# Attention mixer: fp32 operands in one matmul instead of three, and second Fourier step, pool projection and the first output products inside the attention's steps

## The chip, the cores and the metric

One core of one Trainium2 chip. The metric is the device time of one execution in microseconds (us). Engines are named as in the profile: PE is the matmul engine (PEld its weight loads), DVE the vector engine, ACT the scalar engine, POOL the GpSimd engine, SP the engine that issues the weight transfers.

## The reference, cut to what matters

Two blocks run one after the other on x of 512 tokens by 1024 channels. The first block has two layers of feed-forward, mixer, feed-forward; the change touches only its mixer:

```
p = rmsnorm(x) @ w_in[l]                 # 2048 columns: a 256, f 256, q 512, k 512, v 512
y_pool = pool_mixer(a, pool_w, pool_scale)          # window means, then a 64x64 product per group
y_four = real(fft2(f)) @ fourier_w                  # over 64 channels, then over 512 tokens
for each of 4 heads and both halves j of 64 channels:
    s = q_j k_j^T / 8 - slope * |i - t|;  p_j = softmax(s)
o = (p_0 - lam * p_1) @ v;  y_attn = rmsnorm(o over the head's 128) * (1 - lam_init)
x = x + concat(y_pool, y_four, y_attn) @ w_out
```

The second block (memory, block and dilated attention) is not touched.

## The kernel before

**Products.** Activations lie feature-major in SBUF (128 channels by 512 tokens a tile). A product of fp32 data is made from split operands: `x_hi` is x rounded to fp32r, `x_lo` the rest, and the helper `three` issues hi*hi, hi*lo and lo*hi as three fp32r matmuls (lines 439 to 441). Plain fp32 matmuls stand in a few places only, such as the means over channels (L459, L659) and the transposes (L640).

**Weights.** All weights come as panels of 128x2048 through two slots. SP loads `raw`, ACT writes `w_hi` in two halves (L888, `split`), POOL writes `w_lo` in four quarters (L431), and PE waits in `panel(p)`. ACT may only split panel p+2 when PE is done with panel p (`split_after(p, s)`), so a panel that follows a short one comes late.

**The mixer, first stage.** `MIX_ORDER` lists 24 "units", each one PSUM bank of 128x512: a, f, q, fc (first Fourier step, over channels), k, yf (second Fourier step, over tokens, two panels, 48 matmuls), v, four (the Fourier weights), pool. A unit goes through four banks in turn; PE waits in `free_bank(i)` until unit i-4 is out. Every unit is read by ACT (`unit_hi`) and by DVE (`unit_lo`); for a, f, q, k, v DVE first multiplies by the reciprocal norm into `hraw`, then ACT makes the hi part, then DVE the lo part. On ACT the same loop also holds the panel splits, in the order of the units. `pool_block` (DVE) stands ahead of q 2 and of k 1. The vectors fc share their tiles with v.

**The mixer, attention.** 16 pairs (head h, block b of 128 queries) run through a software pipeline; the loop counts steps s:

- PE in step s: scores of s (halves j=0 and j=1 on rows 0 to 63 and 64 to 127 of the array, into bank pair `2 * (s % 2) + j`), transposes of s-3, every second step the outputs of two pairs (v times at), each fourth step the sum for the head norm (L659).
- ACT in step s: in some steps the square of a head's output, or the `guesses` for its norm (a table load, three operations; the next Exp loads its table again), then Exp of s, sometimes the next head's bias, then `at_hi` of s-3 (L1067).
- DVE in step s: bias and maximum of s (L1467, then `nmx` L1471, which releases `s_max`), the combination `att` of s-1 (L1477 to L1482), `at_lo` of s-3 (L1264), and for four steps the head norm (`newton`, L1495, L1498, L1264).

After the last step come the output products: `project_out` goes through 4 panels with two output tiles each (j, g), 8 contraction tiles k each, and waits for head k-4 at k >= 4 of the first. Its results go to x on DVE (L1317), and the second feed-forward begins.

## Time and profile before

| | |
|---|---|
| median of 3 runs | 2718.3 us (2717.61 to 2718.39) |
| the profiled execution | 2716.47 us, of which the span of its instructions is 2714.5 |
| PE busy | 2507.8 us, 92% of the span |
| DVE, ACT, POOL busy | 1259.7, 1108.5, 1116.9 us |
| granted TensorE clock, mean | 0.966 of full |

The shares are means over stages that differ: the page's slices show PE at 9 or 10 tenths in the feed-forwards and at 6 or 7 in the slices of the two mixers. A row of the timeline gives start (us), duration (us), engine, line, operation, output<-inputs, shape, count, and in brackets the idle time ahead of it and who ended it. A row of the windows gives the stretch, its length, then for each engine the busy us and in parentheses the instructions, then the granted clock of TensorE (0.50 is 1.2 GHz, 1.00 is 2.4 GHz), the share of the DMA engines and GB/s.

### The profile page before, as it was taken

The numbers are of one execution on the slowest core, as the hardware profiler recorded it, in microseconds if no ns is written. First come the engines' busy times: TensorE is split into PE (matmuls) and PEld (weight loads), VectorE is DVE, ScalarE is ACT, GpSimd is POOL, SyncE is SP. The second block draws the span as 40 slices with busy tenths as digits, with TensorE's granted clock in tenths as the row PEclk, the third lists the DMA queues.
The fourth block names the chain that finished last, engine by engine and source line by source line (L and its number), as shares of the span: only waits on it lengthen the run. The fifth ranks groups of instructions, "written<-read, shape, count | busy, mean of one in ns | idle before, by whom it ended". The sixth has DMA issues, their size and how long they took to land.

```text
span 2714.5 us, 31002 instructions
## 1 busy us (share of the span) xinstructions
PE 2507.8 (92%) x11290; PEld 2011.8 (74%) x11290; DVE 1259.7 (46%) x2005; ACT 1108.5 (41%) x1616; POOL 1116.9 (41%) x828
## 2 busy tenths in 40 slices
PE   6999999769999999999999589999999997899977
PEld 5888787547888788887887367887887675777756
DVE  5444025563444115443044745444067756566662
ACT  4333133453333224332143534332146665456662
POOL 4455445304545445544445114554443231433222
PEclk9999999879999999999999789999999998999999
DMA  3222222202222222222223002222232221122211
GB/s 147 97 102 93 93 99 102 93 1 78 95 106 93 93 93 93 93 98 96 97 103 114 33 32 93 93 93 93 93 140 74 74 78 39 69 95 64 77 55 62
DMA packets 37470, 233.25 MB, mean 86 GB/s; under 512 B 5632, under 2 KB 5632, under 8 KB 10624
## 3 DMA queue, kind: packets, MB, share of 16 engines
q1 hardware_dynamic: 35424, 224.42, 23.7%
q10 hardware_dynamic: 1952, 7.54, 0.7%
q8 instruction: 63, 1.03, 0.2%
q14 instruction: 31, 0.25, 0.0%
HBM read 223.55 MB, written 2.10 MB: 83 GB/s over the span
## 4 chain that ended last, share of the span: by engine, by line
issue 61%; POOL 38%; POOLq 1%
POOL w_lo L431 38%; POOLq L425 0%; POOLq L429 0%; POOLq L202 0%; POOLq L431 0%; POOLq L1823 0%
## 5 line engine op out<-in xcount | busy, mean ns | idle before, releaser
L431 POOL TENSOR_TENSOR w_lo<-raw,w_hi 128x512 fp32r<-128x512 f32 x824 | 1116.7, 1387 | 1597.1 <-ACT w_hi L888 1596.8
L439 PE MATMUL ps<-h_hi,w_hi 128*128 128x512 f32 x2304 | 924.5, 401 | 36.9 <-DVE h_lo L1264 15.0
L441 PE MATMUL ps<-h_hi,w_lo 128*128 128x512 f32 x2304 | 904.6, 393 | 0.0
L440 PE MATMUL ps<-h_lo,w_hi 128*128 128x512 f32 x2304 | 904.5, 393 | 0.0
L888 ACT ACTIVATE w_hi<-raw 128x1024 fp32r<-128x1024 f32 x412 | 413.5, 1052 | 862.9 <-PE ps L441 855.3
L439 PEld LDWEIGHTS ps<-h_hi,w_hi 128*128 128x128 f32 x2304 | 438.1, 190 | 136.5 <-issue 18.6
L440 PEld LDWEIGHTS ps<-h_lo,w_hi 128*128 128x128 f32 x2304 | 438.4, 190 | 93.3 <-issue 5.3
L441 PEld LDWEIGHTS ps<-h_hi,w_lo 128*128 128x128 f32 x2304 | 437.1, 190 | 93.4
L439 PE MATMUL ps<-hid_hi,w_hi 128*128 128x512 f32 x704 | 279.6, 397 | 7.5 <-DVE hid_lo L1264 7.5
L441 PE MATMUL ps<-hid_hi,w_lo 128*128 128x512 f32 x704 | 278.7, 396 | 0.0
L440 PE MATMUL ps<-hid_lo,w_hi 128*128 128x512 f32 x704 | 278.3, 395 | 0.0
L1317 DVE SCALAR_TENSOR_TENSOR x_sb<-ps,x_sb 128x512 f32<-128x512 f32 x64 | 43.6, 686 | 451.1 <-PE ps L441 451.1
L1336 DVE TENSOR_TENSOR sq<-hraw,sq 128x512 f32<-128x512 f32 x88 | 139.7, 1588 | 222.6 <-ACT hraw L975 222.6
L888 ACT ACT_TABLE_LOAD x42 | 53.9, 1283 | 320.3 <-PE ps L441 315.7
L439 PEld LDWEIGHTS ps<-hid_hi,w_hi 128*128 128x128 f32 x704 | 132.6, 188 | 41.0 <-DVE hid_lo L1264 9.2
L1332 DVE TENSOR_TENSOR hraw<-ps,guess 128x512 f32<-128x512 f32 x88 | 60.8, 691 | 213.2 <-PE ps L441 212.4
L441 PEld LDWEIGHTS ps<-hid_hi,w_lo 128*128 128x128 f32 x704 | 132.6, 188 | 32.7
L440 PEld LDWEIGHTS ps<-hid_lo,w_hi 128*128 128x128 f32 x704 | 132.4, 188 | 32.0
L1338 DVE CAST hid_hi<-sq 128x512 f32 (+1 forms) x88 | 111.3, 1264 | 14.7 <-issue 14.5
L1264 DVE TENSOR_TENSOR hid_lo<-sq,hid_hi 128x512 f32 (+1 forms) x88 | 100.6, 1143 | 12.6 <-issue 0.2
L748 PE MATMUL ps<-cst,att 128*128 128x128 f32 x304 | 52.7, 309 | 36.9 <-ACT att L1132 35.0
L1124 ACT ACTIVATE pt_hi<-ps 128x256 fp32r<-128x256 f32 (+2 forms) x64 | 43.2, 675 | 106.6 <-PE ps L748 106.1
(267 smaller groups left out, 2482.5 us busy)
## 6 DMA issues: line engine op xcount, KB each, us to landing
raw<-in_stream SPq DMA_DIRECT2D x206, 1024.0 KB, 4.8
hraw<-xs SPq DMA_DIRECT2D x96, 64.0 KB, 2.0
x_sb<-in_x ACTq DMA_DIRECT2D x1, 2048.0 KB, 10.5
out_x<-x_sb SPq DMA_DIRECT2D x8, 256.0 KB, 2.7
mem_sb<-in_mem ACTq DMA_DIRECT2D x1, 1024.0 KB, 13.3
rec_sb<-in_recip ACTq DMA_DIRECT2D x2, 512.0 KB, 4.7
memn<-in_mem ACTq DMA_DIRECT2D x1, 1024.0 KB, 4.8
dist_sb<-in_dist ACTq DMA_DIRECT2D x2, 448.0 KB, 3.1
```

The lines of the kernel that those rows point to most:

```text
L431: ins = gp.tensor_tensor(w_lo[:, s, c], raw[:, s, c], w_hi[:, s, c].bitcast(F32), ALU.subtract)
L439: pe.matmul(dst, l_hi, r_hi, start=first, stop=False)
L440: pe.matmul(dst, l_hi, r_lo, start=False, stop=False)
L441: return pe.matmul(dst, l_lo, r_hi, start=False, stop=last)
L748: mm = pe.transpose(dst, src, const(C_ID))
L888: act.activation(w_hi[:, s, c], raw[:, s, c], ACT.Copy).then_inc(hi_split, 1)
L1124: act.activation(pt_hi[:, :, 0:kbs, P * b:P * b + P], src, ACT.Copy).then_inc(t_thi, 1)
L1264: return dve.tensor_tensor(dst, src, hi.bitcast(F32), ALU.subtract)
L1317: dve.scalar_tensor_tensor(out=x_sb[:, m, :], in0=ps[:, m, :], scalar=scale, in1=x_sb[:, m, :], op0=ALU.mult, op1=ALU.add).then_inc(x_read ...
L1332: dve.tensor_tensor(hraw[:, e, :], ps[:, 2 * e, :], rstd, ALU.mult).then_inc(gate_in, 1)
L1336: dve.tensor_tensor(sq[:, e, :], hraw[:, e, :], sq[:, e, :], ALU.mult)
L1338: dve.tensor_copy(hid_hi[:, c, :], sq[:, e:e + 1, :])
```

## The change

Queries, keys, values and probabilities stay fp32 and unsplit (`q_sb`, `k_sb`, `v_sb`, `at_sb`): one fp32 matmul stands where three fp32r ones stood, DVE writes q, k and v alone, and `at_lo` is gone. `fc` gets tiles of its own. The order of the stream becomes v ahead of yf, and the units yf, pool, four (20 to 25, `BEFORE1` = 20) leave the first stage: PE does them in pieces at the end of the attention's steps 0 to 11 (`fill`), into banks 2 and 3. For that the scores have one pair of banks (0 and 1) instead of two, and PE waits for the maximum of s-1 ahead of the scores of s. ACT and DVE take the hi and lo part of a finished unit in the step after (6, 8, 9, 10, 11, 12); the splits of panels 11, 12 and 13 of the mixer's stream move into ACT's steps 4, 8 and 12. In steps 16, 17, 18 and 20 `fill` issues the products k = 0 to 6 of the first two output tiles, and `project_out` begins there with k = 7.

The order of the units:

```
-    + [("yf", c, 8 if c else None) for c in range(2)]
-    + [("v", t, 10 if t == 3 else None) for t in range(4)]
-    + [("four", c, None) for c in range(2)]
-    + [("pool", c, 11 if c else None) for c in range(2)]
+    + [("v", t, 8 if t == 3 else None) for t in range(4)]
+    + [("yf", c, 10 if c else None) for c in range(2)]
+    + [("pool", c, None) for c in range(2)]
+    + [("four", c, 11 if c else None) for c in range(2)]
...
+BEFORE1 = 20
+MIX_UNITS = [(kind, c, i % 4 if i < BEFORE1 else 2 + c, ends) for i, (kind, c, ends) in enumerate(MIX_ORDER)]
+
+FILL_STEPS = {5: 20, 7: 21, 8: 22, 9: 23, 10: 24, 11: 25}
```

The matmul engine:

```
+                def yf(e, c, ts):
+                    w = [t[:, e, :].rearrange("p (t n) -> p t n", t=TB) for t in (w_hi, w_lo)]
+                    s = slice(256 * c + P * e, 256 * c + P * e + P)
+                    for t in ts:
+                        mm = three(ps[:, 2 + c, :], fc_hi[:, t, s], fc_lo[:, t, s],
+                                   w[0][:, t, :], w[1][:, t, :], e == 0 and t == 0, e == 1 and t == TB - 1)
+                    return mm
+
+                def fill(s):
+                    if s < 8:
+                        e, c, ts = s // 4, s // 2 % 2, range(2 * (s % 2), 2 * (s % 2) + 2)
+                        if s % 4 == 0:
+                            panel(p0 + 9 + e)
+                        mm = yf(e, c, ts)
+                        if s == 3:
+                            mm.then_inc(panel_done, 1)
+                    elif s < 10:
+                        c = s - 8
+                        if c == 0:
+                            panel(p0 + 11)
+                        pe.wait_ge(unit_lo, lo0 + 21 + c)
+                        pe.wait_ge(pooled, 2 * l + c + 1)
+                        w = slice(512 + P * c, 512 + P * c + P)
+                        mm = three(ps[:, 2 + c, :], w_hi[:, 0, w], w_lo[:, 0, w],
+                                   m_hi[:, c, :], m_lo[:, c, :], True, True)
+                    elif s < 12:
+                        c = s - 10
+                        pe.wait_ge(unit_lo, lo0 + 23 + c)
+                        for k in range(2):
+                            w = slice(256 * k + P * c, 256 * k + P * c + P)
+                            mm = three(ps[:, 2 + c, :], w_hi[:, 0, w], w_lo[:, 0, w],
+                                       f_hi[:, k, :], f_lo[:, k, :], k == 0, k == 1)
+                    elif UNITS1 <= s <= UNITS1 + 4 and s != UNITS1 + 3:
+                        ks = {UNITS1: (0, 1), UNITS1 + 1: (2, 3), UNITS1 + 2: (4, 5), UNITS1 + 4: (6,)}[s]
+                        if s == UNITS1:
+                            panel(p0 + MIX_PANELS)
+                            pe.wait_ge(s_max, u0 + UNITS1)
+                            pe.wait_ge(unit_lo, lo0 + NU)
+                        for k in ks:
+                            if k >= 4:
+                                pe.wait_ge(s_y, HEADS1 * l + k - 3)
+                            for g in range(2):
+                                project(0, g, 1, k, k)
+                    if s in FILL_STEPS:
+                        finish(FILL_STEPS[s], mm)
...
-                        if s >= 2:
-                            pe.wait_ge(s_max, u0 + s - 1)
+                        if s >= 1:
+                            pe.wait_ge(s_max, u0 + s)
                         for j in range(2):
                             r, c = slice(64 * j, 64 * j + 64), slice(P * b, P * b + P)
-                            mm = three(ps[:, 2 * (s % 2) + j, :], q_hi[r, h, c], q_lo[r, h, c],
-                                       k_hi[r, h, :], k_lo[r, h, :], True, True)
+                            mm = pe.matmul(ps[:, j, :], q_sb[r, h, c], k_sb[r, h, :], start=True, stop=True)
...
-                            mm = three(ps[:, 6 + h % 2, q], v_hi[:, kb, c], v_lo[:, kb, c],
-                                       at_hi[:, kb, q], at_lo[:, kb, q], kb == 0, kb == TB - 1)
+                            mm = pe.matmul(ps[:, 6 + h % 2, q], v_sb[:, kb, c], at_sb[:, kb, q],
+                                           start=kb == 0, stop=kb == TB - 1)
...
+                    fill(s)
+                project_out(p0 + MIX_PANELS, 1, lambda k: pe.wait_ge(s_y, HEADS1 * l + k - 3),
+                            begun=(KB - 1, 0, 0, 0))
```

The scalar engine, at the end of its step s:

```
+                    if s - 1 in FILL_STEPS:
+                        i = FILL_STEPS[s - 1]
+                        unit_high(i)
+                        if MIX_UNITS[i][3] is not None:
+                            split_after(p0 + MIX_UNITS[i][3], (MIX_UNITS[i][3] + 1) % 2)
+                    if s == 4:
+                        split_after(p0 + 9, 0)
```

The vector engine, for q and k, and in its step s:

```
+                        ins = dve.scalar_tensor_tensor(out=(q_sb if kind == "q" else k_sb)[:, c, :], in0=src,
+                                                       scalar=0.125 if kind == "q" else 1.0,
+                                                       in1=rstd, op0=ALU.mult, op1=ALU.mult)
...
-                        remainder(at_lo[:, :, q], ps[:, 4 + u % 2, :].rearrange("p (k n) -> p k n", k=TB),
-                                  at_hi[:, :, q]).then_inc(s_tlo, 1)
+                    if s - 1 in FILL_STEPS:
+                        unit_low(FILL_STEPS[s - 1])
```

**ACT in the first stage.** The engine ACT from the first unit q on, before (L1031 is the hi part of a unit, L888 a half of a panel's split):

```order
L1031 ACTIVATE q_hi<-hraw 128x512
L888 ACTIVATE w_hi<-raw 128x1024 x2
L1031 ACTIVATE q_hi<-hraw 128x512 x2
L888 ACTIVATE w_hi<-raw 128x1024 x2
L1031 ACTIVATE q_hi<-hraw 128x512
L1031 ACTIVATE v_hi<-ps 128x512 x3
L888 ACTIVATE w_hi<-raw 128x1024 x2
```

and ACT at the same place now (L903 is the split, L1036 the hi part):

```order
L1036 ACTIVATE f_hi<-hraw 128x512
L903 ACTIVATE w_hi<-raw 128x1024 x4
L1036 ACTIVATE fc_hi<-ps 128x512 x3
L903 ACTIVATE w_hi<-raw 128x1024 x2
L1036 ACTIVATE fc_hi<-ps 128x512
```

The hi parts of q are gone, and with them the place of the second split behind the third q.

**PE in a step of the attention.** The engine PE in step 5, before (L439 to L441 the scores, L640 the transposes):

```order
L439 MATMUL ps<-k_hi,q_hi 128x512
L440 MATMUL ps<-k_lo,q_hi 128x512
L441 MATMUL ps<-k_hi,q_lo 128x512
L439 MATMUL ps<-k_hi,q_hi 128x512
L440 MATMUL ps<-k_lo,q_hi 128x512
L441 MATMUL ps<-k_hi,q_lo 128x512
L640 MATMUL ps<-cst,att 128x128 x4
```

and PE in step 5 now, with the scores, transposes and outputs of step 6 behind it (L646, L654, L665):

```order
L646 MATMUL ps<-k_sb,q_sb 128x512 x2
L654 MATMUL ps<-cst,att 128x128 x4
L440 MATMUL ps<-w_hi,fc_hi 128x512
L441 MATMUL ps<-w_lo,fc_hi 128x512
L442 MATMUL ps<-w_hi,fc_lo 128x512
L440 MATMUL ps<-w_hi,fc_hi 128x512
L441 MATMUL ps<-w_lo,fc_hi 128x512
L442 MATMUL ps<-w_hi,fc_lo 128x512
L646 MATMUL ps<-k_sb,q_sb 128x512 x2
L654 MATMUL ps<-cst,att 128x128 x4
L665 MATMUL ps<-at_sb,v_sb 128x256 x4
```

Six matmuls of the second Fourier step came in behind the transposes, and the next scores stand behind them.

**DVE in a step.** The engine DVE in a step of the attention before, from the maximum on (ISA rows are the maximum's operation and its read):

```order
L1471 TENSOR_SCALAR nmx<-mx 128x2
L1477 RECIPROCAL rsum<-ssum 128x2
L1479 TENSOR_SCALAR att<-prob,rsum 128x512
L1480 TENSOR_TENSOR rsum<-rsum,nlam_all 128x1
L1482 SCALAR_TENSOR_TENSOR att<-prob,rsum,att 128x512
L1264 TENSOR_TENSOR at_lo<-ps,at_hi 128x4x128
```

and DVE in step 6 now:

```order
L1503 TENSOR_SCALAR nmx<-mx 128x2
L1509 RECIPROCAL rsum<-ssum 128x2
L1511 TENSOR_SCALAR att<-prob,rsum 128x512
L1512 TENSOR_TENSOR rsum<-rsum,nlam_all 128x1
L1514 SCALAR_TENSOR_TENSOR att<-prob,rsum,att 128x512
L1283 TENSOR_TENSOR f_lo<-ps,f_hi 128x512
```

At the place of `at_lo`, in six of the steps, stands the lo part of a filled unit; in the others nothing stands there.

## Rows read from the trace of the kernel before

**Rows 1.** Windows: first stage, attention (first layer), two stretches in it, one before.

```profile
394.00:510.60 116.60, 108.27 (x470) 87.66 (x468) 54.09 (x69) 44.11 (x59) 64.67 (x48) 0.97 0.31 108
510.60:608.00 97.40, 62.60 (x285) 42.52 (x285) 68.83 (x196) 53.77 (x108) 4.99 (x4) 0.72 0.06 22
515.00:535.50 20.50, 14.29 (x58) 9.21 (x54) 15.27 (x52) 13.07 (x30) 0.80 (x1) 0.50 0.15 52
535.50:549.10 13.60, 6.23 (x44) 4.23 (x42) 10.56 (x34) 6.94 (x17) 0.00 (x0) 1.00 0.00 1
444.80:450.10 5.30, 5.27 (x12) 4.13 (x13) 0.69 (x1) 1.19 (x2) 4.92 (x4) 0.50 0.58 198
```

**Rows 2.** Timeline, DVE and ACT, one step of the attention and one early step.

```profile
519.27 0.06 DVE L1465 MEMSET tick<- 128x1 f32 x1
522.52 0.06 DVE L1465 MEMSET tick<- 128x1 f32 x1
...
540.34 0.69 DVE L1467 CUSTOM_DVE_ANT_0 prob<-ps,bias 128x512 f32<-128x512 f32 x1
543.36 0.57 ACT L1067 ACTIVATE at_hi<-ps 128x512 fp32r<-128x512 f32 x1
544.58 0.69 DVE L1467 CUSTOM_DVE_ANT_0 prob<-ps,bias 128x512 f32<-128x512 f32 x1
```

**Rows 3.** Timeline, PE: first matmul of yf, of v, of the scores; transposes.

```profile
469.21 0.39 PE L439 MATMUL ps<-w_hi,v_hi 128*128 128x512 f32 x1
481.80 0.40 PE L439 MATMUL ps<-w_hi,h_hi 128*128 128x512 f32 x1
510.62 0.50 PE L439 MATMUL ps<-k_hi,q_hi 64*128 64x512 f32 x2 [1.56 <-DVE h_lo L1452]
540.57 0.63 PE L640 MATMUL ps<-cst,att 128*128 128x128 f32 x4 [1.88 <-DVE at_lo L1264]
```

**Rows 4.** Timeline, ACT and PE, at the panel after fc.

```profile
436.41 0.28 PE L439 MATMUL ps<-w_hi,f_hi 128*128 128x256 f32 x1
438.22 1.99 ACT L888 ACTIVATE w_hi<-raw 128x1024 fp32r<-128x1024 f32 x2
444.83 0.79 PE L439 MATMUL ps<-h_hi,w_hi 128*128 128x512 f32 x1 [1.37 <-POOL w_lo L431]
```

**Rows 5.** Timeline, ACT and DVE, from the end of v to the first maximum.

```profile
503.79 2.01 ACT L888 ACTIVATE w_hi<-raw 128x1024 fp32r<-128x1024 f32 x2 [1.30 <-PE ps L441]
509.68 1.99 ACT L888 ACTIVATE w_hi<-raw 128x1024 fp32r<-128x1024 f32 x2
512.65 0.06 DVE L1465 MEMSET tick<- 128x1 f32 x1 [2.09 <-ACT bias L1038]
```

**Rows 6.** Timeline, DVE: first nmx, a head norm, the last operation of the heads.

```profile
514.09 0.49 DVE L1471 TENSOR_SCALAR nmx<-mx 128x2 f32<-128x2 f32 x1
565.43 0.68 DVE L1257 SCALAR_TENSOR_TENSOR newt<-ms,newt 128x512 f32<-128x512 f32 x1
568.91 0.69 DVE L1467 CUSTOM_DVE_ANT_0 prob<-ps,bias 128x512 f32<-128x512 f32 x1
607.86 0.69 DVE L1264 TENSOR_TENSOR h_lo<-hraw,h_hi 128x512 fp32r<-128x512 f32 x1
```

**Rows 7.** Timeline, ACT: a head's guesses, to the next Exp.

```profile
553.25 1.28 ACT L898 ACT_TABLE_LOAD   x1
557.83 0.72 ACT L1056 ACTIVATE prob<-prob,nmx 128x512 f32<-128x512 f32 x1
```

**Rows 8.** Timeline, PE: an fp32 mean over 512 columns among fp32r matmuls.

```profile
36.30 1.02 PE L459 MATMUL ps<-sq,cst 128*128 128x512 f32 x2
37.40 0.40 PE L440 MATMUL ps<-h_lo,w_hi 128*128 128x512 f32 x1
37.63 0.40 PE L441 MATMUL ps<-h_hi,w_lo 128*128 128x512 f32 x1
```

**Rows 9.** One tile's group: k_lo, nanoseconds min/median/max.

```profile
L1264 DVE TENSOR_TENSOR k_lo<-hraw,k_hi x8: 693/694/1679, 454.5 to 1461.5; 128x512 fp32r<-128x512 f32 x8
```

More of the change, by code:

```diff
@@ L572, in mixer1 @@
                     i = feature_major(i, j)
[L574 to L587 removed]
                 for j in range(2):
[L589 removed]
+                    panel(p0 + 7 + j)
                     w = [t[:, j, :].rearrange("p (k n) -> p k n", k=KB // 2) for t in (w_hi, w_lo)]
@@ L1000, in mixer1, with unit_high @@
                 act.dma_start(rec_sb[:].rearrange("p a n -> p (a n)"), recip).then_inc(in_mix, 16)
[L1001 to L1007 removed]
+                def unit_high(i):
+                    kind, c, bank, ends = MIX_UNITS[i]
                     if kind in NORMED:
@@ L1031, in mixer1 @@
                     act.activation(dst, src, ACT.Copy, scale=scale).then_inc(unit_hi, 1)
-                    if (kind, c) == ("pool", 1):
+                for i in range(BEFORE1):
+                    kind, c, bank, ends = MIX_UNITS[i]
+                    if (kind, c) == ("v", 0):
+                        split_after(p0 + 7, 0)
+                    if ends is not None and (kind, c) != ("a", 1):
                         split_after(p0 + ends, (ends + 1) % 2)
+                    if kind not in WHOLE:
+                        unit_high(i)
                 def head_bias(h):
```

172 lines of the change are left out of this document (62 added, 110 removed).

## The prediction

> **What bounds the kernel now.** I read the page's slices first: the matmul engine is the bound in the feed-forwards and loses its density in two places only, the mixers. The windows then split the first layer's mixer [rows 1]. In the first stage, 116.6 us, PE is busy for 108.3: PE bounds it. In the attention, 97.4 us, PE is busy for 62.6 and at a mean clock of 0.72, while DVE has 68.8. Work that leaves the first stage shortens it at PE's price, and work put into the attention costs nothing as long as the chain of DVE and ACT sets the step. The second layer repeats both stages (the head norms, softmax and splits have the same counts), so I work one layer and double it.
>
> The timeline shows that chain. A late step lasts from the maximum at 540.34 to the next at 544.58, 4.24 us [rows 2]: maximum and nmx (1.4), two Exps, at_hi at 543.36 (0.57), at_lo until 544.58 (0.65). DVE waits in it for ACT. An early step, before any at_lo exists, goes from 519.27 to 522.52, 3.25 us: there DVE alone is the bound. PE is free for half of either.
>
> **Matmuls, price of one.** Two fp32r matmuls of 512 columns start 0.23 us apart at the full clock; a plain fp32 one pushes its successor: from 36.30 to 37.40 lie it and one fp32r, so it takes 0.87 [rows 8]. Three fp32r cost 0.69. Unsplitting therefore does not save PE time, it costs a quarter more. For 256 columns (outputs) I take half, 0.43 against 0.35, an estimate from the same rows. The halves of the scores run side by side on their 64 rows [rows 3] (x2 in 0.50); no row shows this for fp32. I take it as the same (pair about 1.0 us); the other end is one after the other, 1.9. What the unsplit form saves is on DVE and ACT: at_lo, and the lo and hi parts of q, k, v.
>
> **First stage, what goes.**
> - yf, from 481.80 back to 469.21 [rows 3], 12.6 us, with one late panel in it. It moves whole into the steps; v follows k, and its two panels of 48 matmuls (10.9 us) each cover the supply of the next.
> - The panel after fc. ACT's second split begins at 438.22, behind the hi part of a q that waited for the window sums; PE began fc, so was done with that panel, at 436.41 [rows 4]. Now nothing stands ahead of it: 1.6 us earlier at 436.6. PE's two other stalls there go, but it then waits for this panel until 444.83 - 1.6. I take 1.6. Ends: 0, and 4.2 if the low clock behind the gap [rows 1] (last row, 12 matmuls in 5.3 us, half speed) goes as well.
> - From the end of v to the first maximum: 503.79 to 512.65, 8.9 us, today with four and pool in it. Now ACT does one split and the first bias, the same two as from 509.68 to 512.65, 3.0 us [rows 5]; DVE's v 3 and PE's first scores, together some 2 us, go beside it. Saved: 5.9.
>
> Sum: 20.1 us a layer. Into the steps go 66 matmuls of fill, 15 us of PE.
>
> **The steps, from the first nmx (514.09) to the last head's lo part (607.86 + 0.69): 94.5 us now** [rows 6]. Worked interval by interval, first up to the fourteenth nmx:
> - To the third nmx 6.6 as now: the table load of the first Exp sets it.
> - Steps without a fill's lo part are DVE's 3.25 instead of 4.24. PE fits at the full clock: transposes 0.6 [rows 3] and six fill matmuls 1.4 run beside the maximum, the next scores (1.0) beside att. Four such intervals, 13.0.
> - Steps 6, 8, 9, 10, 11, 12 keep the old chain, with a hi part put in (0.53) and the unit's lo in the place of at_lo: 4.24 + 0.53 = 4.77. This is where much of the gain stops.
> - Splits of 2.0 us [rows 5] stand on ACT behind steps 4, 8 and 12. The last two end about when the next nmx does. The one in step 4 makes the Exp of 5 late and through it step 6: 5.2 instead of 4.8. Step 8 has a bias too (some 0.8, what rows 5 leave beside the split; 5.6), step 9 a square (5.1).
> - The guesses and the table back take 4.6 us ahead of Exp (553.25 to 557.83) [rows 7]. In step 10, with ACT free 2.1 us ahead of nmx, they delay Exp by 2.3: 7.1. Step 11 holds the first norm, 565.43 to 568.91, 3.5 [rows 6]: 8.3.
> - With 3.3 for step 7 and 4.8 for step 12: 59.0.
> - POOL. Today it is quiet here, 5.0 us in 97 [rows 1]; now it makes three more panels, 5.0 us each, next to att, whose operands all lie in SBUF. Such an operation takes 0.69 alone and 1.68 at most [rows 9]; in the timeline the long ones are those that meet POOL. Each panel meets one att, two such operations and two small ones: +2.2, of which the waits for ACT absorb about half up to here. I add 2.2: 61.2.
>
> Then the tail: guesses, Exp 14, att 14, norm (3.5), att 15, transposes, outputs. The third panel's meeting costs 2 at step 14. PE now has 12 product matmuls (2.7) behind each of steps 16, 17, 18, and the last outputs stand behind them. Followed through, from the fourteenth nmx: second norm ends at 14.0, outputs of step 16 at 11.0, products to 13.7, step 17 to 17.8, step 18 to 22.7, outputs to 24.5, k = 6 to 25.9, sum 26.9, guesses 29.1, norm 32.6.
>
> 61.2 + 32.6 = 93.8 against 94.5: **the steps gain 0.7 us only, but carry the fills.**
>
> **Behind it** PE has 150 matmuls left up to the end of the products instead of 171, at 0.227: 4.8 us saved. The later panels are ready (ACT 2 and POOL 5.0 against 10.9 of work).
>
> **Sum:** 20.1 + 0.7 + 4.8 = 25.6 a layer, 51 in all. The profiled execution took 2716.5, so 2665.5; the median of the runs shown lies 1.8 above it. **I predict 2667.**
>
> **Two rules weighed.** The Trainium skill (SBUF — State Buffer, the summary of the port rules) says that the pair of ports which DVE and GpSimd share is an exclusive lock, taken by a DVE instruction with two SBUF inputs for its whole length, the other blocked. By that rule an att operation could wait for a whole POOL operation, 1.25 us (a quarter of the 5.0 in rows 1), instead of the 0.99 of k_lo, and the sum would be up to 3 us worse. I stay with the measured 0.99. The Trainium skill (TensorE: Matmul & The Clock Gate, Part 4) also says that transposes do not count as work for the clock; by it, steps 12 to 15, which hold no fill, would run at 1.2 GHz, about 4 us a layer more (scores and outputs at twice their time). No row here separates this from plain idleness.
>
> **Rivals.**
> - **Scores one after the other (0.15).** If plain fp32 does not run side by side, a pair takes 1.9 and the short steps grow from 3.25 to about 3.7, the even steps with outputs by some 0.8, because there is only one pair of banks: 7 us a layer, **2681**. For it: no fp32 row of 64 rows exists. Against: the fp32r rows.
> - **Deeper gain (0.14).** The low clock behind fc goes (2.6), POOL hardly meets att (3), and PE's ends come earlier: 6 to 8 a layer more, **2653**.
> - **PE becomes the bound at 1.2 GHz: slower (0.05).** At half the clock everything doubles: a step with fill and outputs costs PE 1.9 + 1.1 + 3.4 + 2.8 = 9.2, one without outputs 5.8. Over the steps that is 83 us instead of 61, in the tail the products cost 9.5 more, and outputs and sums 7: 39 a layer, **2745**. It decides when more than two thirds of the attention is at the low clock. For it: from 515.0 to 535.5 the clock stayed at 0.50 with PE busy for 70% of the time [rows 1]. Against: behind 444.8, with PE busy without a gap, it was back after 5.3 us, and from 535.5 it held for 13.6 us at 46% busy. A PE that is the bound is busy without a gap, so the state ends itself.
> - **The fills only change places (0.02).** If each fill lengthened the chain by its own time, 15 us of yf, pool and four and 9.5 of products, the 25.6 would shrink to 1 a layer: **2716**, no change. Against: DVE and ACT, not PE, end the waits in the attention.
> - The forecast itself has 0.64.
>
> **Range.** The forecast's unknowns are the stall behind fc (0 to 4.2 a layer), POOL (0 to 8), low clock in steps without fills (0 to 4): 2655 to 2681 for itself. With the deeper gain and the serial scores (and some low clock on top of them), 8 in 10 reaches from 2648 to 2690. A measurement of this kernel tells 0.2%, 5.4 us, from no change. Faster 0.93, same 0.02, slower 0.05.
>
> **What the changed profile would show.** v begins where yf did, at about 467.5; the first maximum is near 492.6; the fourteenth nmx about 61 us behind the first; in steps 6, 8 to 12 DVE's lo part waits for ACT's hi part; short steps 3.25 apart; the first matmul behind the last h_lo is followed by 149 more. Wrong if: two score halves start 0.9 apart; PE has no gaps in the steps and the clock there is under 0.7; nmx to nmx in steps 3 to 5 exceeds 4 us; or att takes over 1.6 us in more steps than the three with a panel.

## The result, and the profile after

The changed kernel takes 2670.75 us (median of 4 runs, 2669.8 to 2671.66) against 2718.22; the ratio is 0.9826, with an interval from 0.9809 to 0.9843. The prediction was 2667. The profiled execution took 2671.64 us, its span 2669.8.

Where the 44.7 us of the span come from, first layer. "First stage" goes from the first panel's mean to the first nmx, "steps" to the fourteenth nmx, "tail" to the end of the last head's h_lo, "behind" to the next mean. nmx is the negated row maximum, one a step; an interval is the time from one nmx to the next, counted from the first. The table holds every kernel of this study, so that the experiments below can be read against it:

| kernel | first stage | steps | tail | behind | median, us |
|---|---|---|---|---|---|
| before | 111.70 | 60.44 | 34.02 | 51.78 | 2718.2 |
| after | 90.25 | 60.04 | 34.48 | 48.41 | 2670.8 |
| products_behind | 90.29 | 60.05 | 32.75 | 51.78 | 2671.1 |
| products_late | 90.28 | 60.03 | 30.42 | 47.07 | 2662.1 |
| low_later | 90.27 | 58.00 | 37.56 | 49.85 | 2668.1 |
| fills_before | 111.76 | 53.22 | 35.49 | 49.24 | 2706.2 |
| splits_later | 90.28 | 64.40 | 38.28 | 49.53 | 2685.3 |
| at_lo_back | 90.29 | 65.73 | 37.35 | 49.10 | 2692.1 |
| single_fp32r | 90.28 | 59.99 | 31.63 | 48.50 | 2662.8 |
| combo | 90.28 | 59.75 | 32.51 | 47.09 | 2667.8 |
| behind_scores | 90.26 | 60.06 | 35.35 | 49.65 | 2670.8 |
| behind_late | 90.27 | 60.03 | 30.15 | 47.08 | 2660.2 |
| behind_late_low | 90.25 | 58.34 | 31.01 | 47.07 | 2657.5 |
| splits_12_18 | 90.25 | 53.95 | 33.84 | 47.07 | 2649.9 |

The median of one kernel is known less sharply than the stages: the executions of a kernel differ by up to 11.4 us (behind_late, 2653.57 to 2665), each ratio below carries an interval of about 4 us to either side, and the stage columns come from one profiled execution each. Medians 2 or 3 us apart are not told apart here.

The windows of after that answer to [rows 1]: first stage, attention, its first five steps, the stretch in steps 12 to 14 at 1.2 GHz, and two short stretches, one in a feed-forward and one behind the last h_lo.

```profile
394.00:494.10 100.10, 95.87 (x426) 78.19 (x425) 39.56 (x56) 31.75 (x39) 49.33 (x38) 0.98 0.30 108
494.10:590.10 96.00, 74.44 (x301) 44.81 (x299) 71.64 (x186) 60.63 (x117) 18.82 (x15) 0.91 0.12 44
494.10:511.00 16.90, 14.28 (x62) 7.50 (x61) 13.93 (x48) 10.64 (x24) 3.11 (x3) 1.00 0.16 63
548.70:562.40 13.70, 9.33 (x21) 3.87 (x22) 11.89 (x31) 11.23 (x19) 5.12 (x4) 0.50 0.10 32
275.60:279.10 3.50, 3.50 (x11) 2.69 (x10) 0.29 (x1) 0.00 (x0) 0.00 (x0) 0.51 0.83 300
590.00:593.10 3.10, 2.90 (x7) 2.36 (x8) 0.74 (x2) 0.00 (x0) 0.00 (x0) 0.50 0.00 0
```

In the attention PE is busy for 11.8 us more than before, and the attention lasts as long (nmx to last h_lo 94.5 in both). Its clock is 0.91 where it was 0.72. The fills are only part of that, as fills_before shows below; in the first five steps, which hold five of the eight fills of yf, they are the larger part, and there it ran at 1.00.

PE's rows that answer to [rows 3, 4], at the panel after fc, the first v and the first scores:

```profile
445.66 0.50 PE L440 MATMUL ps<-h_hi,w_hi 128*128 128x512 f32 x1 [3.39 <-POOL w_lo L432]
469.15 0.39 PE L440 MATMUL ps<-w_hi,h_hi 128*128 128x512 f32 x1
491.92 1.13 PE L646 MATMUL ps<-k_sb,q_sb 64*128 64x512 f32 x4 [0.84 <-DVE v_sb L1445]
```

The last row settles the rival of the serial scores: one pair of plain fp32 halves (x4, since each is recorded twice) takes 1.13 us, not 1.9, so they run side by side. On DVE, early steps, the norm in step 11, and att beside a POOL operation:

```profile
495.54 0.48 DVE L1503 TENSOR_SCALAR nmx<-mx 128x2 f32<-128x2 f32 x1
500.72 0.06 DVE L1497 MEMSET tick<- 128x1 f32 x1
503.98 0.06 DVE L1497 MEMSET tick<- 128x1 f32 x1
...
545.38 0.69 DVE L1283 TENSOR_TENSOR h_lo<-ps,h_hi 128x512 fp32r<-128x512 f32 x1 [1.00 <-ACT h_hi L1036]
...
555.57 0.29 DVE L1503 TENSOR_SCALAR nmx<-mx 128x2 f32<-128x2 f32 x1
556.00 1.34 DVE L1511 TENSOR_SCALAR att<-prob,rsum 128x512 f32<-128x512 f32 x1
557.26 1.21 DVE L1512 TENSOR_TENSOR rsum<-rsum,nlam_all 128x1 f32<-128x1 f32 x1
558.55 1.68 DVE L1514 SCALAR_TENSOR_TENSOR att<-prob,rsum,att 128x512 f32<-128x512 f32 x1
562.14 0.49 DVE L1511 TENSOR_SCALAR att<-prob,rsum 128x512 f32<-128x512 f32 x1
562.54 0.15 DVE L1512 TENSOR_TENSOR rsum<-rsum,nlam_all 128x1 f32<-128x1 f32 x1
562.77 0.75 DVE L1514 SCALAR_TENSOR_TENSOR att<-prob,rsum,att 128x512 f32<-128x512 f32 x1
```

A short step is 3.26 us (500.72 to 503.98), as predicted. In a step with a fill the low part waits 1.00 us for ACT's high part, as predicted. And the same three operations of att take 4.23 us beside POOL (at 554.56 it begins the four quarters of a panel's low part, 5.12 us) and 1.39 alone: one such meeting costs DVE 2.8 us. The end of the attention on PE:

```profile
577.39 0.58 PE L440 MATMUL ps<-h_hi,w_hi 128*128 128x512 f32 x1
580.33 1.89 PE L665 MATMUL ps<-at_sb,v_sb 128*128 128x256 f32 x8
583.43 1.02 PE L673 MATMUL ps<-sq,cst 128*128 128x512 f32 x2
590.20 0.77 PE L440 MATMUL ps<-h_hi,w_hi 128*128 128x512 f32 x1 [5.74 <-DVE h_lo L1283]
590.76 0.63 PE L441 MATMUL ps<-h_lo,w_hi 128*128 128x512 f32 x1
```

The products of step 18 (from 577.39) stand ahead of the last outputs (580.33), as the prediction had it. What it gave no price is what comes next: PE waits 5.74 us for the last head, and starts again at 1.2 GHz (0.50 in the last window above). Nor did it ask what the tail would be without these products.

### The profile page after: what moved, and what is told of

The parts are those of the page before. It is cut to its first block, busy times and chain, and to the rows that moved or that the text cites. A ratio compares the mean times of both kernels' runs of the same rounds, so it can differ in the third digit from the quotient of the medians.

```text
span 2669.8 us, 30642 instructions
## 1 busy us (share of the span) xinstructions
PE 2496.9 (94%) x11162; PEld 1988.4 (74%) x11162; DVE 1230.3 (46%) x1949; ACT 1093.4 (41%) x1592; POOL 1114.6 (42%) x828
## 4 chain that ended last, share of the span: by engine, by line
issue 61%; POOL 39%; POOLq 1%
POOL w_lo L432 39%; POOLq L426 0%; POOLq L430 0%; POOLq L207 0%; POOLq L432 0%; POOLq L1851 0%
## 5 line engine op out<-in xcount | busy, mean ns | idle before, releaser
L441 PE MATMUL ps<-h_lo,w_hi 128*128 128x512 f32 x2304 | 905.8, 393 | 0.0
L903 ACT ACTIVATE w_hi<-raw 128x1024 fp32r<-128x1024 f32 x412 | 413.5, 1052 | 924.1 <-PE ps L442 916.6
L441 PEld LDWEIGHTS ps<-h_lo,w_hi 128*128 128x128 f32 x2304 | 439.1, 191 | 93.5 <-issue 5.3
L441 PE MATMUL ps<-hid_lo,w_hi 128*128 128x512 f32 x704 | 279.5, 397 | 0.0
L441 PEld LDWEIGHTS ps<-hid_lo,w_hi 128*128 128x128 f32 x704 | 133.0, 189 | 33.3
L1283 DVE TENSOR_TENSOR hid_lo<-sq,hid_hi 128x512 f32 (+1 forms) x88 | 100.5, 1143 | 12.6 <-issue 0.2
```

The source lines that it names most:

```text
L441: pe.matmul(dst, l_hi, r_lo, start=False, stop=False)
L903: act.activation(w_hi[:, s, c], raw[:, s, c], ACT.Copy).then_inc(hi_split, 1)
L1283: return dve.tensor_tensor(dst, src, hi.bitcast(F32), ALU.subtract)
```

## The experiments

**Where the early products stand.** First, none of them early (`fill` loses its branch for steps 16 to 20, `begun` goes):

```
-                project_out(p0 + MIX_PANELS, 1, lambda k: pe.wait_ge(s_y, HEADS1 * l + k - 3),
-                            begun=(KB - 1, 0, 0, 0))
+                pe.wait_ge(s_max, u0 + UNITS1)
+                pe.wait_ge(unit_lo, lo0 + NU)
+                project_out(p0 + MIX_PANELS, 1, lambda k: pe.wait_ge(s_y, HEADS1 * l + max(k - 3, 1)))
```

> The changed kernel, but no output product is begun inside the attention's last steps: all 150 matmuls more or less, 192 minus nothing, stand behind the last steps again, in the order k = 0 to 7 for the first two output tiles. Theory (the products only filled idle time and lengthened nothing): the 42 early matmuls come back behind the heads, but k = 0 to 6 of them can still run while the last head's norm is made, since they wait for earlier heads alone; they then cover the 5.7 us in which the matmul engine now idles there, the clock stays high, and the last outputs come 2.7 us earlier because no product stands ahead of them. So the kernel is faster or equal: 0 to 4 us a layer, 2663 to 2671 us. Rival (the early products were worth the 4.8 us a layer that the prediction gave them): slower by about 9.6 us, 2680.

Measured 2671.12 us, ratio 0.9827 (0.9813 to 0.984): the same as the changed kernel. The table shows why: "behind" goes back to 51.78, the tail shrinks by 1.7. In the second layer 1.8 us behind stand against 1.8 in the tail. What the 21 matmuls saved behind the last h_lo, they cost ahead of it and in clock, all of it in the second layer and all but 1.6 us in the first. (Only the first output tile's k = 0 to 6 can cover the wait when each tile is done in turn.) The second kernel keeps them early but out of the way:

```
+PRODUCTS = {16: (0,), 17: (1,), 20: (2,), 21: (3, 4, 5, 6)}
...
-                    elif UNITS1 <= s <= UNITS1 + 4 and s != UNITS1 + 3:
-                        ks = {UNITS1: (0, 1), UNITS1 + 1: (2, 3), UNITS1 + 2: (4, 5), UNITS1 + 4: (6,)}[s]
+                    elif s in PRODUCTS:
+                        ks = PRODUCTS[s]
```

> The changed kernel with the early products spread otherwise: k = 0 in step 16, k = 1 in 17, k = 2 behind the last outputs in step 20, k = 3 to 6 in step 21 behind the head's sum. Theory (the products of step 18 held the last outputs back, and the idle time ahead of the last h_lo cost the clock): the last outputs start some 2.4 us earlier, and k = 3 to 6 (5.5 us) lie in the idle 5.7 us, so that the next matmuls run at full clock: 1.4 us (layer 0) and 3 us (layer 1) less. Together 3.8 to 5.4 us a layer, 2661 to 2663 us. Rival (the wait of the last outputs is set by the transposes and ACT, not by the products ahead of them): only the clock's part, 2666 to 2668.

Measured 2662.13 us, ratio 0.9799 (0.9785 to 0.9812). PE of this kernel at the sum of the last head and at the first matmul behind it:

```profile
577.79 1.02 PE L674 MATMUL ps<-sq,cst 128*128 128x512 f32 x2
...
584.57 0.47 PE L441 MATMUL ps<-h_hi,w_hi 128*128 128x512 f32 x1 [0.26 <-DVE h_lo L1284]
584.87 0.40 PE L442 MATMUL ps<-h_lo,w_hi 128*128 128x512 f32 x1
585.10 0.39 PE L443 MATMUL ps<-h_hi,w_lo 128*128 128x512 f32 x1
```

The wait is 0.26 us instead of 5.74 and the next matmuls start 0.30 and then 0.23 us apart. Tail 4.1 and behind 1.3 us shorter: the theory held, and the same 42 matmuls are now worth 9 us instead of nothing.

**What the moved units are worth.** yf, pool and four (6 of the units of `MIX_ORDER`, which are 26 and not 24) ahead of the attention again, into the four banks in turn; early products as in the changed kernel:

```
-                pe.wait_ge(unit_lo, lo0 + BEFORE1)
+                for s in range(12):
+                    if s in (0, 2):
+                        pe.wait_ge(unit_lo, lo0 + 17 + s // 2)
+                    fill(s)
+                pe.wait_ge(unit_lo, lo0 + NU)
...
-                    fill(s)
+                    if s >= UNITS1:
+                        fill(s)
```

> The changed kernel with its unsplit fp32 operands, but the second Fourier step, the pool projection and the Fourier weights (66 matmuls) done ahead of the attention again; the early output products stay. It tells what the moved work is worth with unsplit operands. Theory of the prediction: the first stage gets back some 17 to 18 us a layer (48 matmuls 11 us, 18 more 4, the wait from the last unit to the first maximum); the steps lose their low parts, high parts, splits and the meetings with POOL: eleven intervals of 3.3, one of 3.3 + 3.5 for the norm, one with 2.3 for the guesses, 49 instead of 60 us, so 11 back. Net 6 to 7 us a layer slower: 2683 to 2685. Rival A (the fills are nearly free in the steps): slower by 15 or more a layer, over 2700. Rival B (the fills cost in the steps what they take in the first stage): within 2 us a layer of the changed kernel, 2667 to 2675.

Measured 2706.21 us, ratio 0.9961 (0.9948 to 0.9975). In the first layer the first stage is 21.5 us longer, that is as long as before, and the steps give back only 6.8, where 11 were expected (tail and behind are 1.8 longer). That is outside the theory's 2683 to 2685 and in the range of rival A: the fills are nearly free. Its first stage, its attention, the early steps and the later ones:

```profile
394.00:512.80 118.80, 109.59 (x476) 88.22 (x474) 41.38 (x57) 39.40 (x49) 65.74 (x51) 0.97 0.33 115
512.80:604.00 91.20, 62.48 (x241) 35.36 (x240) 59.19 (x180) 52.09 (x105) 1.76 (x2) 0.86 0.04 12
512.80:532.00 19.20, 12.51 (x34) 4.16 (x32) 13.48 (x48) 10.89 (x24) 1.76 (x2) 0.57 0.16 55
532.00:567.80 35.80, 23.84 (x99) 12.49 (x100) 27.25 (x89) 22.90 (x50) 0.00 (x0) 0.95 0.00 1
```

Without fills the early steps run at 0.57 of the clock; with scores at 1.2 GHz a step lasts 3.74 us (513.25 to 516.99 between maxima), not 3.3. So the fills pay part of their own way: they keep the clock there. Over the whole attention the clock is 0.86 without any fill, against 0.72 before the change and 0.91 with them, so most of the rise in the mean comes with the rest of the change. The run is also the measure of the change's parts: what is left without the moved units (unsplit operands and early products) gives 12 us of the 47, and the moved units 35.

**What at_lo was worth.** An operation of its size back on DVE, into scratch:

```
+                        dve.wait_ge(s_thi, u0 + u + 1)
...
+                        dve.tensor_tensor((hraw, sq)[u % 2][:, 1, :].rearrange("p (k n) -> p k n", k=TB),
+                                          ps[:, 4 + u % 2, :].rearrange("p (k n) -> p k n", k=TB),
+                                          at_sb[:, :, P * b:P * b + P], ALU.subtract).then_inc(s_tlo, 1)
...
-                            pe.wait_ge(s_thi, u0 + u - 1)
+                            pe.wait_ge(s_tlo, u0 + u - 1)
```

> The changed kernel with an operation of the size and place of the old at_lo put back on DVE, 16 a layer, after ACT's copy of the transposed probabilities; its result goes to scratch and PE's transposes wait for it as before. It tells what the missing at_lo is worth. Theory of the prediction (at_lo closed the step): intervals without a filled unit grow from 3.3 to 4.24, five of them up to the fourteenth nmx, 4.7; the six with one grow by 0.65, 3.9; the tail by 2: 10 to 11 us a layer, 2691 to 2693. Rival (in the steps with a filled unit ACT or PE's queue closes the step and DVE has room): 6 to 7 a layer, 2683 to 2685.

Measured 2692.09 us, ratio 0.9903 (0.9888 to 0.9918), 21 us slower than the changed kernel. The mixers hold 9.3 and 8.7 of it, 18 us; the rest lies outside them. In the first layer the steps are 5.7 us longer and the tail 2.9. The fourth interval, a short step, is 4.24 us instead of 3.32:

```profile
507.93 0.69 DVE L1524 TENSOR_TENSOR hraw<-ps,at_sb 128x512 f32<-128x512 f32 x1 [0.51 <-ACT at_sb L1080]
508.55 0.69 DVE L1500 CUSTOM_DVE_ANT_0 prob<-ps,bias 128x512 f32<-128x512 f32 x1
```

DVE waits for ACT's copy and does its operation, and only then comes the maximum. The total came as the prediction's theory had it, but partly by chance: the mixers' 9.3 and 8.7 lie between its 10 to 11 and the rival's 6 to 7, and what lies outside them fills the gap. The steps grew by 5.7 instead of 8.6, and the tail by more than 2. The intervals with a filled unit did have room: the seventh and the ninth to thirteenth together did not grow, the fourth, fifth, sixth and eighth grew by 6.

**What plain fp32 costs on PE.** q, k, v and probabilities rounded to fp32r, one matmul each; their low parts are left out:

```
-        q_sb = sb("q_sb", [P, HEADS1, T], F32, mix)
+        q_sb = sb("q_sb", [P, HEADS1, T], F32R, mix)
```

(and the same for k_sb, v_sb, at_sb)

> The changed kernel with q, k, v and the probabilities rounded to fp32r and one fp32r matmul where a plain fp32 one stands (the low parts of these four are left out of the computation). It tells what fp32's price on PE is worth: scores 1.13 us a pair, outputs 1.9. Theory (PE has room in the short steps; its time counts only where the next scores stand behind outputs or the sum, in intervals 9 to 11, and for the last outputs): 0.5 to 1 us at each of 4 or 5 places, 2 to 4 us a layer, 2663 to 2667. Rival A (hidden everywhere): 2670 to 2672. Rival B (scores are on the chain of every step): 16 times 0.5 us and more, 8 or more a layer, under 2656.

Measured 2662.78 us, ratio 0.9794 (0.9781 to 0.9807). A pair of scores now takes 0.50 us, four matmuls of outputs 0.64 instead of 1.89:

```profile
496.40 0.50 PE L646 MATMUL ps<-k_sb,q_sb 64*128 64x512 f32 x2
...
576.85 0.64 PE L665 MATMUL ps<-at_sb,v_sb 128*128 128x256 f32 x4
```

But the steps take 59.99 us against 60.04. What the mixers gain is in the tail, 2.9 us in the first layer and 3.0 in the second. PE's price is hidden in every interval up to the fourteenth nmx; the theory had the size nearly right (2662.8 against 2663 to 2667) and the place half wrong, since I had also expected something of intervals 9 to 11. The lighter PE was also at the low clock for longer (0.83 over the attention, 494 to 585, against 0.91), so the two kernels do not differ in fp32's price alone.

**What closes the intervals behind step 8.** Seven kernels. DVE's low part one step later, behind nmx:

```
                         dve.tensor_scalar(nmx[:, s % 2, :], mx[:, s % 2, :], -1.0, None, ALU.mult).then_inc(s_max, 1)
+                    if s - 2 in FILL_STEPS:
+                        unit_low(FILL_STEPS[s - 2])
...
-                    if s - 1 in FILL_STEPS:
-                        unit_low(FILL_STEPS[s - 1])
```

> The changed kernel, but DVE makes the low part of a filled unit one step later, right behind that step's nmx, so that it does not wait for ACT's high part of the same step. Theory (in steps 6 and 8 to 12 DVE waits for ACT's high part, and that wait closes the step): DVE then needs 3.25 + 0.7 = 3.95 us in such a step and ACT sets the sum of the five steps 8 to 12 by its own work: 5 times (1.4 Exp + 0.57 + 0.53) + bias 0.8 + two splits 4.0 + square 0.6 + guesses 4.6 = 22.5 us, where 30.7 are measured; as waits stay between them I expect 3 to 5 us less a layer, 2661 to 2665 us. Rival (ACT itself is full in these steps, so the step only waits elsewhere, ahead of att instead of ahead of the next maximum): within 1 us a layer, 2669 to 2673. A loss would mean that att, now 0.7 us later, is what sets the transposes.

Measured 2668.11 us, ratio 0.9811 (0.9798 to 0.9825), between the 2661 to 2665 of the theory and the 2669 to 2673 of the rival. 2.0 us less in the steps of either layer, but in the profiled execution the two mixers together take as long as those of the changed kernel: in the first layer the tail is 3.1 us longer. The seventh interval falls from 5.40 to 4.80 and the ninth from 5.56 to 3.30, but the tenth grows from 6.65 to 8.23. In it PE waits 3.83 us for ACT's square ahead of the sum (528.75), and the fill and the next scores stand behind that, the scores at 1.2 GHz (2.08 us). ACT's two splits elsewhere:

```
-                        if MIX_UNITS[i][3] is not None:
-                            split_after(p0 + MIX_UNITS[i][3], (MIX_UNITS[i][3] + 1) % 2)
...
+                    if s == 11:
+                        split_after(p0 + 10, 1)
+                    if s == 15:
+                        split_after(p0 + 11, 0)
```

> The changed kernel, but ACT splits the first two panels of the output products behind its steps 11 and 15, in which DVE makes a head norm, not behind steps 8 and 12. Nothing needs these panels before step 16. Theory (ACT's split ahead of the head's square holds up PE's queue: the sum for the head norm waits for the square, and the next scores stand behind the sum): the interval from the tenth to the eleventh nmx shrinks from 6.65 by up to the 2.0 us of the split, to 4.7 to 5.2, and the fourteenth to fifteenth from 6.2 to 4.5; 3 to 3.7 us a layer, 2664 to 2666 us. Rival (ACT's two microseconds only turn up elsewhere, in step 12 and the tail): within 1 us a layer, 2669 to 2673.

Measured 2685.26 us, ratio 0.9879 (0.9863 to 0.9894): 14 us slower, neither theory. The tenth interval did fall, from 6.65 to 4.87. The eleventh rose from 5.53 to 9.79 and the twelfth from 8.20 to 10.07:

```profile
534.48 3.75 PE L665 MATMUL ps<-at_sb,v_sb 128*128 128x256 f32 x8 [4.22 <-ACT newt L916]
...
547.04 1.59 DVE L1280 SCALAR_TENSOR_TENSOR guess<-newt,guess 128x512 f32<-128x512 f32 x1
...
550.12 1.59 DVE L1285 TENSOR_TENSOR h_lo<-hraw,h_hi 128x512 fp32r<-128x512 f32 x1
```

PE came to its wait for the guesses earlier, was idle for 4.22 us and did the outputs at 1.2 GHz (3.75 us instead of 1.97), with a fill, partly at 1.2 GHz too, and the next scores behind them. And POOL, 6.18 us from 546.66 on, now lay on the head norm, 1.59 us instead of 0.69 for two of its operations. Low parts, splits (11 and 15) and late products together:

> The changed kernel with three edits together: early products spread as in the run that put them late, low parts one step later behind nmx, and the two splits behind steps 11 and 15. The first gave 8.7 us, the second 2.6; the theory says that the second was held back by the split ahead of the square (an interval of 8.2 us there), so that with the third edit the two give more than apart: 2671.1 less 8.7, 2.6, 6 to 7 and 2 to 4 more, 2649 to 2654 us. Rival (each removes the same wait): 2658 to 2662.

Measured 2667.84 us, ratio 0.9815 (0.9801 to 0.9828), outside the theory's 2649 to 2654 and the rival's 2658 to 2662, and worse than late products alone: the splits' place costs more than the low parts give. The loss is in the eleventh interval again, 9.04 us, the one with the outputs of step 10 ahead of the scores. The twelfth, with the head norm, is 8.25: POOL began at 543.84 and met one large operation of the norm, the last (1.59 us). Then the order on PE: sums of steps 9 and 13 and outputs of 10 and 14 behind the next scores:

```
+                def comes_late(s):
+                    return s in (9, 10, 13, 14)
...
                         mm.then_inc(s_scores, 1)
+                    if comes_late(s - 1):
+                        outputs(s - 1)
+                        head_sum(s - 1)
...
+                    if not comes_late(s):
+                        outputs(s)
+                        head_sum(s)
```

> The changed kernel, but on PE the two things that wait for ACT around a head's end stand behind the next scores: the head's sums of steps 9 and 13 and the outputs of steps 10 and 14. Queue theory (the scores stand behind a wait that is not theirs, 3.3 us ahead of the sum and 0.9 ahead of the outputs, and that closes intervals 10 and 11, 6.65 and 5.53 us): if the scores alone set them, each shrinks by 1 to 2 us, 4 to 6 us over both heads' ends in a layer, 2660 to 2664 us. ACT theory (ACT is busy without a gap from step 8's Exp to step 10's high part, and DVE's low part waits for that): the tenth interval shrinks and the eleventh takes it back; within 1 us a layer, 2669 to 2672.

Measured 2670.8 us, ratio 0.9826 (0.9812 to 0.984): nothing. Scores 10 (PE) and the low part, nmx (DVE) of this kernel:

```profile
528.41 1.13 PE L671 MATMUL ps<-k_sb,q_sb 64*128 64x512 f32 x4 [0.64 <-DVE nmx L1516]
...
532.66 0.74 DVE L1484 SCALAR_TENSOR_TENSOR h_lo<-ps,v_all,h_hi 128x512 fp32r<-128x512 f32 x1
...
534.71 0.17 DVE L1516 TENSOR_SCALAR nmx<-mx 128x2 f32<-128x2 f32 x1
```

The scores are ready by 529.5, and the maximum still comes behind the low part. So the queue on PE was not the last wait there. DVE of the changed kernel in the same interval:

```profile
530.48 0.29 DVE L1503 TENSOR_SCALAR nmx<-mx 128x2 f32<-128x2 f32 x1
530.68 0.15 DVE L1509 RECIPROCAL rsum<-ssum 128x2 f32<-128x2 f32 x1
530.91 1.34 DVE L1511 TENSOR_SCALAR att<-prob,rsum 128x512 f32<-128x512 f32 x1
532.17 1.23 DVE L1512 TENSOR_TENSOR rsum<-rsum,nlam_all 128x1 f32<-128x1 f32 x1
533.48 1.68 DVE L1514 SCALAR_TENSOR_TENSOR att<-prob,rsum,att 128x512 f32<-128x512 f32 x1
535.08 0.74 DVE L1471 SCALAR_TENSOR_TENSOR h_lo<-ps,v_all,h_hi 128x512 fp32r<-128x512 f32 x1
```

It is busy without a gap, with att beside POOL (the second panel's four quarters begin at 529.47). So the ACT theory had the number and not the whole cause: POOL's meeting fills the interval whether ACT is late or not. (The eleventh stays at 5.53: there the low part waits 1.73 us for ACT's high part.) The same with late products:

> The run before it together with the early products spread late (k = 0 in step 16, 1 in 17, 2 in 20, 3 to 6 in 21), which alone gave 2662.1. If the two touch different waits the gains add up: ACT theory 2660 to 2663, queue theory 2651 to 2655. A sum much above that would mean that the low clock of the tail moved onto the products.

Measured 2660.18 us (2653.57 to 2665), ratio 0.9792 (0.9778 to 0.9806): as late products alone within the spread, the intervals unchanged. With the low parts later as well:

> The run before it together with the low parts one step later behind nmx. Theory: the low parts free DVE from ACT's high part (alone 2.6 us, since PE's queue then held the scores, an interval of 8.2 us), the order on PE frees the scores; with both, only ACT's own work is left between the ninth and twelfth nmx: Exp 11 follows the high part at once (2.3 us idle there with the low parts alone), and the intervals 9 to 12 fall from 25.9 us to 21 to 23. 2 to 4 us a layer below the run before it if that one is at 2661: 2653 to 2657. Rival (ACT has no room left, the head's guesses with their two table loads set it): 2658 to 2662.

Measured 2657.49 us, ratio 0.9767 (0.9753 to 0.9781); its interval overlaps that of the run before it. The tenth interval is 6.07 where the low parts alone had 8.23, but the eleventh takes it back, 7.89 where they had 6.12. The intervals 9 to 12 come to 25.1 us, not 21 to 23, and the steps of the first layer to 58.34, where the low parts alone gave 58.00; only in the second layer is there a gain, 56.19 against 58.36. What stretches the eleventh, on DVE and PE:

```profile
529.73 1.24 DVE L1528 TENSOR_TENSOR rsum<-rsum,nlam_all 128x1 f32<-128x1 f32 x1
531.04 1.69 DVE L1530 SCALAR_TENSOR_TENSOR att<-prob,rsum,att 128x512 f32<-128x512 f32 x1
...
535.82 0.80 PE L441 MATMUL ps<-f_hi,w_hi 128*128 128x512 f32 x1 [3.07 <-DVE h_lo L1485]
...
538.68 2.08 PE L672 MATMUL ps<-k_sb,q_sb 64*128 64x512 f32 x4
```

POOL, working on the panel that ACT split behind step 8, meets att 9; the low part comes late; PE waits 3.07 us for it and then does the fill and the scores at 1.2 GHz (2.08 us instead of 1.13). Last, then, the splits again, in steps 12 and 18:

```
+                    if s == 12:
+                        split_after(p0 + 10, 1)
+                    if s == 18:
+                        split_after(p0 + 11, 0)
```

> The run before it (products late, sums and outputs behind the next scores, low parts a step later) with ACT's splits of the first two panels of the output products behind its steps 12 and 18 instead of 8 and 12. It tests why the run with them behind steps 11 and 15 lost 14 us. Theory: there the split itself was well placed (the tenth interval fell by 1.8 us), but POOL's low part came to lie on the head norms, 10.07 us instead of 8.20 twice a layer, and PE's idle time ahead of the outputs of step 10 brought it to 1.2 GHz (9.8 us instead of 5.5). In steps 12 and 18 POOL meets att 12 and 13 and the third norm, on which nothing waits but k = 6. Expected: the intervals of steps 9 and 10 lose 2 to 3 us, 2 to 3 us a layer, 2651 to 2655 us. Rival (any shift of POOL or of ACT's 2 us is paid back elsewhere): 2656 to 2660. If the low clock is what costs there, idle PE ahead of step 10's outputs makes it over 2660.

Measured 2649.86 us (2649.38 to 2652.06), ratio 0.9753 (0.9739 to 0.9766), below the whole range expected. Window of its attention, and PE at scores 10, the sum behind them, and scores 11:

```profile
493.50:584.00 90.50, 73.78 (x309) 46.54 (x310) 70.20 (x183) 61.48 (x118) 17.86 (x14) 0.96 0.13 47
```

```profile
528.01 1.13 PE L672 MATMUL ps<-k_sb,q_sb 64*128 64x512 f32 x4
529.07 1.12 PE L659 MATMUL ps<-sq,cst 128*128 128x512 f32 x2
...
533.06 1.13 PE L672 MATMUL ps<-k_sb,q_sb 64*128 64x512 f32 x4
534.12 1.99 PE L649 MATMUL ps<-at_sb,v_sb 128*128 128x256 f32 x8
```

The intervals tenth to twelfth are 4.47, 5.04 and 7.94, where the kernel before it has 6.07, 7.89 and 7.88 and the changed kernel 6.65, 5.53 and 8.20. The steps are 6.1 us shorter than the changed kernel's, and the clock is 0.96. The tail is 2.8 us longer than that of the kernel before it: now the outputs of step 14 run at 1.2 GHz (3.78 us from 556.75), and POOL lies on the third head norm (1.60 us for its last operation). This is the fastest kernel of the study, 21 us below the change.

It does not say which half of the theory was right. The run with the splits in steps 11 and 15 differs from this one in the steps and also in the order on PE and the low parts, and its 14 us had two parts: the outputs ahead of the scores, which the order on PE takes away, and POOL on the norm, which the other places of the splits take away from all but the third norm. Neither the splits in 11 and 15 with the new order nor the splits in 12 and 18 alone were run.

## Why the prediction was right, by its own steps

- **First stage, 20.1 a layer: 21.45 measured.** v began at 469.15, where yf had begun, not at 467.5: PE's way from the mean to it shrank by 2.95, more than the 1.6 taken for the panel after fc, but the mean itself came 2.9 later (see the sum). So the terms of the sum came out, and the start named for v did not. From the start of fc to the panel behind it are 6.37 us instead of 8.42, and the low clock behind it lasted 3.4 us. From 469.15 to the first maximum are 24.95 us; before, from the first yf at the same place, 43.44: 18.49 less, against 18.5 (12.6 + 5.9) predicted.
- **Steps, 61.2: 60.04 and 60.39.** Third nmx 6.61 (6.6). Three of the four short steps 3.27 to 3.32 (3.25), the fourth 4.17: the split of step 4 delays its Exp already. Seventh interval 5.40 (5.2), ninth 5.56 (5.6), twelfth 8.20 (8.3), thirteenth 4.72 (4.8). The eleventh was 5.53 where I had 7.1, the tenth 6.65 where I had 5.1 and POOL: the sum of the two, 12.2, was right by chance, since I had put POOL's cost in a lump and the guesses where ACT had no room. POOL cost 2.8 a meeting, not 2.2 (the operation on one column had been booked at next to nothing). at_lo_back showed what the lighter step is worth, single_fp32r that PE has room.
- **Tail, 32.6: 34.48 and 34.2.** The last outputs started 24.8 us behind the fourteenth nmx, not 22.7, although the prediction had put the products of step 18 ahead of them. The second norm already ended at 16.0 instead of 14.0 and moved what follows; att 12 beside POOL (2.8, not 2) is 0.8 of that, the rest was not taken apart.
- **Behind, 4.8: 3.37 and 1.86.** I counted 21 matmuls and no clock. The predicted row, the first matmul behind the last h_lo with 149 more, came, but PE now waits for the last head with nothing left to do, and the first matmuls pay for it: 3.4 us at 1.2 GHz in the first layer, 6.8 in the second. That is the step that failed in substance: the prediction booked 4.8 us for the early products and set nothing against them. Without them the tail is 1.7 and 1.8 us shorter, so that after the clock 1.6 us were left of them in the first layer and none in the second, which products_behind showed. In products_late "behind" is 47.07, 4.7 less than before, as the count of matmuls had it.
- **Sum.** Mixers 257.94 to 233.18 and 258.14 to 234.80: 48.1 us, against 51. Terms too low and too high cancel in it: a layer, the first stage gave 1.3 to 1.6 more than its 20.1, and the steps up to the fourteenth nmx took about 1 less than their 61.2; the tail took 1.6 to 1.9 more, and behind it 1.4 and 2.9 of the 4.8 were missing. The span lost 3.4 of the 48.1 outside the mixers, most of it in two stretches such as 275.60 to 279.10, 3.5 us at 0.51, behind an idle PE of 1.83 us. That idle time is in the kernels without such a stretch too. The first feed-forward takes 366.1 or 367.6 us, one or the other, in the kernels of the table, whatever was edited: 367.6 in four (after, products_behind, at_lo_back, behind_late_low), and just these four show a low clock there (0.87 from 270 to 283, all others 1.00). Why the clock falls in one kernel and not in the next stays open; I count this part as scatter.
- **Rivals.** Serial scores: no, 1.13 us a pair. Fills only change places: no, fills_before costs 35 us. PE the bound at 1.2 GHz: no, the clock of the attention is 0.91. Deeper gain: of its first part, 2.6 us, about 1.0 came (behind fc 9 matmuls start in 3.65 us at the low clock, from 446.23 to 449.88, where 12 took 5.3), POOL did meet att, and its size, 2653, was passed only by other orders.
- **The two rules.** The exclusive lock (the Trainium skill, SBUF — State Buffer, "Who interferes with whom"): an operation on 128x1 took 1.21 us beside POOL instead of 0.15, about the 1.25 us of a POOL operation; a large one lost 0.85 to 0.93. So waits of nearly a whole POOL operation occur, as the rule has it. The 0.99 that I stayed with was enough for a large operation; what my price of a meeting lacked is the small one, 1.06 us more. The page names tensor_scalar too, where it runs in a two-port mode, and here TENSOR_SCALAR (0.49 us alone) did lose 0.85. Transposes and the clock (the Trainium skill, TensorE: Matmul & The Clock Gate, Part 4): the steps without fills did fall to 1.2 GHz, from 548.7 to 562.4, in and behind an idle PE of 4.49 us. But two other runs hold steps with transposes and without fills at the full clock, so such steps need not run at 1.2 GHz, as I had worked it out from the rule: fills_before at 0.95 from 532.00 to 567.80, and the last kernel behind its last fill, in the window below. Whether a transpose counts less than another matmul no run separates.

```profile
538.90:553.00 14.10, 7.78 (x35) 3.95 (x34) 13.14 (x27) 9.20 (x17) 5.13 (x4) 1.00 0.00 0
```

## What to carry to other kernels

Work put into another stage's idle time is free only as far as nothing in the same queue behind it is on the chain: give it the places behind the last instruction that others wait for, and keep some of it for the last wait, where it also keeps the clock. When a wait is removed without effect, look at what now ends at the same moment; here DVE beside POOL, ACT's high part and PE's queue closed the same interval. Low parts, order and splits together shortened the steps by 6.1 us; the low parts alone gave 2.0, the order alone nothing, the two together 1.7 in the first layer (the splits in 12 and 18 were not run alone). Ask of each transfer or split that is moved which operation its follower on POOL will meet.

## What the hardware did that I had not expected

- Plain fp32 matmuls on rows 0 to 63 and 64 to 127 overlap like fp32r ones: 1.13 us a pair at the full clock, 2.08 at half, where one fp32 matmul of 512 columns costs 0.87 [rows 8].
- A DVE operation on one column took 1.21 to 1.24 us beside POOL, eight times its 0.15; its neighbours of 512 columns 0.49 to 1.34 and 0.75 to 1.68.
- Fills in idle PE time kept the early steps at the full clock, 1.00 against 0.57 in fills_before. Over the whole attention they matter less: 0.91 against 0.86 (0.72 before the change), and 0.96 in the last kernel, with PE busy for 78%, 69% and 82% of the stretch of after, fills_before and the last kernel.
- The same idle time of PE need not end the same: behind 1.83 us ahead of 275.11 the clock fell to half for one stretch in four of the fourteen kernels, and stayed full in ten.
